# Experts' stage with the sum's turn, residual and final norm taken in, and the last expert's down product split first

## The reference

```python
act = glu * sigmoid(1.702 * glu) * (lin + 1.0)
yb  = (act @ w_down[e] + b_down[e]) * p            # per expert, its tokens
y   = segment_sum(yb)                              # back to the 256 tokens
x   = x + g2 * y
x   = x * rsqrt(mean(x * x) + eps) * final_norm_g  # input of the second block
```

## Time and profile before

| | us |
|---|---|
| median of 3 runs | 3181.67 |
| the profiled execution | 3196.83 |
| its span, first to last instruction | 3195.0 |
| mean granted TensorE clock, share of full | 0.924 |

### The profile page before, as it was taken

One profiled execution on the slowest core, in us unless ns is written; L12 is line 12 of the kernel. 1 busy time (PEld: TensorE's weight loads), 2 busy tenths in 40 slices (PEclk: granted clock), 3 DMA queues, 4 the chain that ended last, 5 costly groups with the idle time before them and its releaser, 6 DMA issues. The chain is left out here.

```text
span 3195.0 us, 43577 instructions
## 1 busy us (share of the span) xinstructions
PE 2973.4 (93%) x17000; PEld 2411.1 (75%) x17001; DVE 2093.8 (66%) x3195; ACT 1608.9 (50%) x2237; POOL 143.4 (4%) x175
## 2 busy tenths in 40 slices
PE   7989999989998879999999999999687899988998
PEld 2458888866767867777777777776685799976998
DVE  2135555534455569999999999997573566574565
ACT  0024444432214358788787887875342445432454
POOL 0023233200000000000000000000000000000000
PEclk9889999998988979999999999999895799985999
DMA  7551010012105489999999999995540255530453
GB/s 260 165 89 34 27 40 14 1 49 73 40 1 150 117 314 381 379 379 381 380 383 379 379 380 378 382 382 201 165 131 1 81 174 175 143 109 1 142 183 125
DMA packets 257848, 604.61 MB, mean 189 GB/s; under 512 B 25987, under 2 KB 82538, under 8 KB 257258
## 3 DMA queue, kind: packets, MB, share of 16 engines
q1 hardware_dynamic: 256556, 601.35, 54.5%
q10 hardware_dynamic: 1085, 0.45, 0.1%
HBM read 596.29 MB, written 5.44 MB: 188 GB/s over the span
## 5 line engine op out<-in xcount | busy, mean ns | idle before, releaser
L2026 DVE TENSOR_TENSOR moe_raw_r<-moe_raw,moe_hi 128x2048 fp32r<-128x2048 f32 x320 | 718.7, 2283 | 10.2 <-ACT moe_hi L1959 10.2
L1959 ACT ACTIVATE moe_hi<-moe_raw 128x2048 fp32r<-128x2048 f32 x320 | 599.7, 1908 | 0.5 <-PE banks L1847 0.5
L2750 PE MATMUL banks<-xs_r,w_hi 128*128 128x272 f32 (+1 forms) x1632 | 475.9, 292 | 25.2 <-DVE w_raw_r L3172 16.6
L2754 PE MATMUL banks<-xs_r,w_raw_r 128*128 128x272 f32 (+1 forms) x1632 | 473.2, 290 | 0.0
L2751 PE MATMUL banks<-xs_r,w_hi 128*128 128x272 f32 (+1 forms) x1632 | 471.0, 289 | 0.0
L2994 ACT ACTIVATE w_hi<-w_raw 128x512 fp32r<-128x512 f32 (+1 forms) x416 | 256.8, 619 | 247.1 <-PE banks L2754 203.4
L2750 PEld LDWEIGHTS banks<-xs_r,w_hi 128*128 128x128 f32 x1632 | 311.9, 191 | 30.3 <-issue 22.3
L2754 PEld LDWEIGHTS banks<-xs_r,w_raw_r 128*128 128x128 f32 x1632 | 312.0, 191 | 3.0
L2751 PEld LDWEIGHTS banks<-xs_r,w_hi 128*128 128x128 f32 x1632 | 312.3, 191 | 0.2
L3172 DVE TENSOR_TENSOR w_raw_r<-w_raw,w_hi 128x512 fp32r<-128x512 f32 (+1 forms) x416 | 271.1, 674 | 57.7 <-ACT w_hi L2994 53.6
L1886 PEld LDWEIGHTS banks<-con,gu_tok 128*128 128x128 f32 x1024 | 191.8, 193 | 30.1 <-ACT gu_tok L1971 9.8
(11 more groups left out here) (484 smaller groups left out, 5523.3 us busy)
## 6 DMA issues: line engine op xcount, KB each, us to landing
moe_raw<-in_w_gu SPq DMA_DIRECT2D x256, 1024.0 KB, 8.4
moe_raw<-in_w_down SPq DMA_DIRECT2D x128, 1024.0 KB, 10.4
w_raw<-in_w_ff SPq DMA_DIRECT2D x256, 256.0 KB, 3.0
w_raw<-in_w_in SPq DMA_DIRECT2D x112, 256.0 KB, 2.7
ring_mod<-in_w_mod SPq DMA_DIRECT2D x12, 2048.0 KB, 8.1
wq<-in_w_in SPq DMA_DIRECT2D x32, 512.0 KB, 4.2
wh<-in_w_in SPq DMA_DIRECT2D x8, 1024.0 KB, 9.5
mg_raw<-in_w_in SPq DMA_DIRECT2D x32, 256.0 KB, 3.0
```

Of the source, the lines that this page charges most:

```text
L1959: act.activation(hi[n % HI_SLOTS][:, :], raw[n % UNITS][:, :], ACT.Copy).then_inc(his, 1)
L2026: dve.tensor_tensor(rest[n % UNITS][:, :], raw[n % UNITS][:, :], hi[n % HI_SLOTS][:, :].bitcast(F32), ALU.subtract).then_inc(los, 1)
L2750: pe.matmul(bank, w_hi, x[:, 0, 0:n_cols], start=first, stop=False)
L2754: ins = pe.matmul(bank, w_lo, x[:, 0, 0:n_cols], start=False, stop=last)
```

## The change

All that the three stages did moves into the experts' stage, behind the last expert:
- The last expert's four units of its down product are rounded and subtracted in one go, on ScalarE ahead of the up sums, on VectorE ahead of `act_first(0)`.
- `scatter` goes through its four products in another order (column half first, token half second) for every expert; in the last one each of the four raises the semaphore.
- The sums are taken out in four parts, two by ScalarE and two by VectorE, each as its product ends; they are turned as before. VectorE adds the residual straight from the turned sums in PSUM, so `yT` and its copies go. The squares go to another buffer (`sum_f`).
- The squares' sum, and the scaling of it, are made ahead of the rare path. Each engine reads the flag earlier (VectorE before the scatter, ScalarE behind the squares, TensorE behind its sum, SyncE behind its last load) and jumps, where no expert overflows, behind that. The rare path itself adds its part to x with a product of its own, and then makes the squares and their sum anew.
- The root's table is loaded behind the squares. A new semaphore `settled`, raised by VectorE behind its jump, releases the root.
- There is one stage end in place of four, with 64 semaphores of its own and 13 held.

The diff, cut to what runs here:

```diff
@@ names of the stage @@
+                 "scat o_hot ... o_act_v o_squared o_summed o_var o_settled y_out_act y_out_dve y_turned fin1_res fin1_sq fin1_sum "
+                 "fin1_var fin1_settled fin1_std fin1_inv " + " ".join(f"o_w{u}" for u in range(UNITS)))
+        def flag_of(eng):
+            return eng.value_load(flags[0:1, 0:1], min_val=0, max_val=NJ)
+
+        def further(eng, some, body):
+            with eng.If(some > 0):
...
+            def last_pe(pe):
+                for i in range(4):
+                    t, c = i % 2, i // 2
+                    pe.wait_ge((out_act, out_dve)[t], c + 1)
+                    for m in range(4):
+                        k = 4 * c + m
+                        ins = pe.transpose(ps[k // 2][:, k % 2 * LAT + t * P:k % 2 * LAT + (t + 1) * P],
+                                           ytok[:, t, k * P:(k + 1) * P], ident)
+                        if t and m % 2:
+                            ins.then_inc(y_turned, 1)
+                pe.wait_ge(res, 2)
+                for k in range(KT):
+                    pe.wait_ge(squared, k + 1)
+                    ins = pe.matmul(ps[0][:, 0:LAT], ones, sq[:, k, :], start=(k == 0), stop=(k == KT - 1))
+                ins.then_inc(summed, 1)
+                some = flag_of(pe)
+                pe.wait_ge(var, 1)
+                further_pe(pe, some)
+
+            def last_act(act):
+                for c in range(2):
+                    act.wait_ge(scat, NEXP + 2 * c)
+                    act.activation(ytok[:, 0, c * 512:(c + 1) * 512], ps[4 + c][:, :], ACT.Copy).then_inc(out_act, 1)
+                for k in range(KT):
+                    act.wait_ge(res, k + 1)
+                    act.activation(sq[:, k, :], xT[:, k, :], ACT.Square).then_inc(squared, 1)
+                some = flag_of(act)
+                act.preload_act_table(ACT.Sqrt)
+                act.wait_ge(var, 1)
+                further_act(act, some)
+                act.wait_ge(settled, 1)
+                act.activation(rinv, rinv, ACT.Sqrt).then_inc(std, 1)
+
+            def last_dve(dve):
+                some = flag_of(dve)
+                for c in range(2):
+                    dve.wait_ge(scat, NEXP + 2 * c + 1)
+                    dve.tensor_copy(ytok[:, 1, c * 512:(c + 1) * 512], ps[6 + c][:, :]).then_inc(out_dve, 1)
+                for k in range(KT):
+                    dve.wait_ge(y_turned, k // 2 + 1)
+                    dve.scalar_tensor_tensor(xT[:, k, :], ps[k // 2][:, k % 2 * LAT:(k % 2 + 1) * LAT], modT[:, 5 * KT + k, 0:1],
+                                             xT[:, k, :], ALU.mult, ALU.add).then_inc(res, 1)
+                dve.wait_ge(summed, 1)
+                dve.tensor_scalar(rinv, ps[0][:, 0:LAT], 1.0 / D, EPS, ALU.mult, ALU.add).then_inc(var, 1)
+                dve.wait_ge(var, 1)
+                further_dve(dve, some)
+                dve.sem_inc(settled, 1)
+                dve.wait_ge(std, 1)
+                dve.reciprocal(rinv, rinv).then_inc(inv, 1)
...
@@ SyncE, behind its last load @@
+                some = flag_of(sp)
+                sp.wait_ge(res, KT)
+                further_sp(sp, some)
@@ scatter @@
-                        t, c = i // 2, i % 2
-                        ins = pe.matmul(ps[4 + i][:, :], pickTs[e % 2][:, t * P:(t + 1) * P], y[:, c * 512:(c + 1) * 512],
+                        t, c = i % 2, i // 2
+                        ins = pe.matmul(ps[4 + 2 * t + c][:, :], pickTs[e % 2][:, t * P:(t + 1) * P], y[:, c * 512:(c + 1) * 512],
-                        if i == 3:
+                        if i == 3 or e == NEXP - 1:
@@ ScalarE, last expert @@
+                    if not nxt:
+                        for q in range(4):
+                            rounded(d0 + q)
+                        out("u", e)
+                        gated(e, 0)
+                        gated(e, 1)
+                        continue
@@ VectorE, last expert @@
+                    if not nxt:
+                        lo(d0, d0 + 1, d0 + 2, d0 + 3)
+                        for h in range(2):
+                            act_first(e, h)
+                            act_second(e, h)
+                        continue
@@ removed: the stages yt, rare path and fin1 (L2078 to L2316) @@
```

More of the change, by code:

```diff
@@ L1779, in experts @@
         hi.append(last_hi)
+        sq = sum_f[:, :].rearrange("p (k t) -> p k t", k=KT)
         pick = sb("pick", [P, 2, 2, 2, 2 * SLOTS], FR)
@@ L1791, in experts @@
         gcur = sb("gate_cur", [P, 2])
+        ytok, rinv = gs, y[:, 0:LAT]
         fold = con[:, K_FOLD:K_FOLD + SLOTS]
@@ new lines, in experts @@
+                 "o_gt_out o_y_out o_sc_mm o_added o_act_v o_squared o_summed o_var o_settled y_out_act y_out_dve y_turned fin1_res fin1_sq fin1_sum "
+                 "fin1_var fin1_settled fin1_std fin1_inv " + " ".join(f"o_w{u}" for u in range(UNITS)))
[3 more added lines that the diff above has]
+            with eng.If(some > 0):
+                with eng.Fori(E_N, NJ) as j:
+                    number = eng.value_load(flags[0:1, bass.ds(j, 1)], min_val=0, max_val=NJ)
+                    with eng.If(number > 0):
+                        item = eng.value_load(items[0:1, bass.ds(j, 1)], min_val=0, max_val=NJ)
+                        body(item, j - E_N if RMAX == 2 else j % E_N, j)
@@ L1951, in _ @@
                         scatter(e)
+                last_pe(pe)
             @block.scalar
@@ L2019, in _ @@
                 results(NEXP - 1)
+                last_act(act)
             @block.vector
@@ L2076, in _ @@
                 dve.wait_ge(x_kept, 32)
[L2078 to L2110, removed]
@@ L2284, in experts @@
-        sq = raw[0][:, :].rearrange("p (k t) -> p k t", k=KT)
-        rinv = y[:, 0:LAT]
-        with stage(nc, "fin1_res fin1_sq fin1_sum fin1_var fin1_std fin1_inv") as (block, res, squared, summed, var, std, inv):
-            @block.vector
-            def _(dve):
-                for k in range(KT):
-                    dve.scalar_tensor_tensor(xT[:, k, :], yT[:, k, :], modT[:, 5 * KT + k, 0:1], xT[:, k, :], ALU.mult, ALU.add)\
-                       .then_inc(res, 1)
-                dve.wait_ge(summed, 1)
-                dve.tensor_scalar(rinv, ps[0][:, 0:LAT], 1.0 / D, EPS, ALU.mult, ALU.add).then_inc(var, 1)
-                dve.wait_ge(std, 1)
-                dve.reciprocal(rinv, rinv).then_inc(inv, 1)
-                dve.wait_ge(res, KT)
-                dve.wait_ge(inv, 1)
-                for k in range(KT):
-                    dve.scalar_tensor_tensor(xT[:, k, :], xT[:, k, :], vec[:, V_FIN + k:V_FIN + k + 1], rinv,
-                                             ALU.mult, ALU.mult)
-            @block.scalar
-            def _(act):
-                act.preload_act_table(ACT.Sqrt)
-                for k in range(KT):
-                    act.wait_ge(res, k + 1)
-                    act.activation(sq[:, k, :], xT[:, k, :], ACT.Square).then_inc(squared, 1)
-                act.wait_ge(var, 1)
-                act.activation(rinv, rinv, ACT.Sqrt).then_inc(std, 1)
-            @block.tensor
-            def _(pe):
-                for k in range(KT):
-                    pe.wait_ge(squared, k + 1)
-                    ins = pe.matmul(ps[0][:, 0:LAT], ones, sq[:, k, :], start=(k == 0), stop=(k == KT - 1))
-                ins.then_inc(summed, 1)
@@ L2319, in route @@
+                last_dve(dve)
 def route(nc, a, ps, con, vec, xT, modT, ident, ones, h_hi, h_lo, rankr, gate, flags, items, first_units):
```

312 lines of the change are left out of this document (162 added, 150 removed).

## The result

The changed kernel takes 3165.96 us (median of 6 runs, 3163.46 to 3173.54), the kernel before 3182.31 in the same comparison (3180.73 to 3186.85). The ratio is 0.995, with a 95% interval of 0.9937 to 0.9963: 12 to 20 us less. The forecast was 13.8 us less, 3168 us. A second comparison gave 3165.8 us and 0.9949 (0.9931 to 0.9967).

What follows compares the result with a forecast made beforehand. From the last expert's scatter each step waits for the one before, engines mostly idle. That stretch falls from 32.97 to 20.35 us (12.6), plus 1.2 in the last expert: 13.8 less, 3168 us, range 3162 to 3177.

Steps and rivals of the forecast that it cites:

- The tail: From the last expert's scatter start to the second block's first VectorE copy: 32.97 us would fall to 20.35.
- Full clock in the sum: TensorE's squares' sum runs at full clock, 0.43 us a step, keeps pace with the squares and ends at 9.0 us.
- its first rival: Half clock in the squares' sum and no clock gain in the down product: 3.4 + 0.6 us back, 3172 us; chance 0.15.
- The stage end: The one end behind the norm, with 20 semaphore clears on VectorE, costs 3.3 us.
- the line: Cost of a stage end on VectorE: 0.67 us and 0.13 more for each semaphore clear.
- The flag: Jump over the rare path on VectorE and ScalarE, between scaling and root: 2.0 us; TensorE's jump 6.4 us, hidden.
- the rival of the free jump: VectorE's jump nearly free, its code at hand; TensorE's jump then sets the end, 1.2 us sooner: 3166.7 us; chance 0.10.
- The last expert: From its first turn to the scatter: activation and down products start sooner, a gain of 1.2 us.
- the prediction's sign: TensorE's down product in the last expert starts 0.8 us behind its turns, not 2.0.
- I take 1.2, as it came back behind each restart here: Last expert's down products: full clock returns as long after the restart as before, so the whole 1.2 us is gained.
- the other value given, 0.6: Last expert's gain in us if TensorE's full clock came back at its old place.
- The slower rival: Second block draws more half clock after starting about 14 us sooner; 60 us more would give 3198 us; chance 0.05.

Runs made afterwards that it cites:

- turn_old: Changed kernel with sums copied out by ScalarE behind the whole scatter, turned sums copied to yT, residual added from there: 3176.2 us, ratio 0.997.
- before_norare: Kernel before without flag, jump and rare-path body, its stage and 31 clears kept: 3177.3 us, ratio 0.9976.
- after_norare: Changed kernel without the rare path, its flag and its jumps: 3162.5 us, ratio 0.9927.
- before_last: Kernel before with only the last expert's new order added: ratio 0.9994 (0.9979 to 1.0009).
- after_lastold: Changed kernel with the last expert's old order put back: 3171.4 us, ratio 0.9964.

## Why the prediction was right, point by point

- **The number**: 13.8 us forecast, 16.4 measured (12 to 20), 3168 against 3165.96 us. The sign, the size and the range held.
- **The tail**: 12.6 forecast, 13.92 in the trace. Two parts of it were tested: the sums taken out by parts and the residual from PSUM (4.2, turn_old), and flag and jump (4.7 before, 0.7 after, so 4.0: before_norare and after_norare). The rest is read from rows and was not tested part by part. The stage ends were 1.79, 2.96 (the two in the middle, from before_norare) and 0.93 in place of 3.13: 2.55 less. From the residual's start to the sum's end it was 7.27 in place of 4.77: 2.5 less, by overlap and by the sum's clock. From the scatter's start to the residual, without the stage end, it was 9.22, and 8.60 in turn_old: 0.6 less. Together that is 13.9.
- **Full clock in the sum** was right, and its first rival falls: 3.69 us in every trace in which TensorE came to the sum without idle time, and in turn_old behind 2.85 us of it. Behind 5.80, 5.90, 10.61 and 10.64 us of idle time it took 5.38, 6.43, 6.17 and 5.56. One sign was missed: the sum ended 1.09 us behind the last square and not within 0.7.
- **The stage end** was right within 0.2 us, and the line holds from 2 to 28 clears on VectorE at 0.12 to 0.13 each; at 28 it gives 4.3, and 4.09 was measured. One premise was wrong without weight in the sum: there are not as many clears before as after, but 72 (19 on VectorE) before and 77 (20) after.
- **The flag was mis-sized**, the largest error of the tail: 2.0 for the jump on VectorE and ScalarE, and 0.80 measured, of which the jump is 0.64. I read the three blocks on q14 as something the engines had waited for. They came behind the root in the changed kernel, and none came between the scaling and the root. That is the rival of the free jump, though at 0.64 it isn't free. That rival's other half was wrong: TensorE's jump did not set the end, since it takes 3.6 us and not 6.4. What I leaned on is the section Instruction fetch mechanics of the page Runtime: NRT & Kernel Launch of the Trainium skill: a taken jump out of the blocks at hand waits for a fetch. For VectorE and ScalarE I misapplied it, since no fetch stands ahead of their restart. On TensorE a block did come 1.3 us into the jump of 3.6, so the trace agrees that there was a fetch; but the engine restarted 2.3 us behind it, and that part is not explained.
- **The last expert**: in before_last the start of the down product moved by 1.23 as forecast, and in all repeats it lay 0.78 us behind the turns, as the prediction's sign has it (1.81 in the changed kernel's first trace). The step that failed is "I take 1.2, as it came back behind each restart here". In the repeats 0.67 was left, nearer to the other value given, 0.6. The changed kernel's first trace has 1.18 by another way: its turns ran at full clock (3.79 in place of 5.56), and the last subtraction became what `act_first(0)` waited for. That it met the 1.2 is luck.
- **The slower rival** did not come. But the second block's length does move by up to 8.6 us between traces, together with its clock, which is over half of the gain, and the prediction had no term for it on the good side.

## What stays open

The medians fell by 16.4 and 18.1 us, the places account for 14.6 (13.9 and 0.7). The difference is within the intervals. That the last expert's order, worth 0.7 us in its place, goes with 5.6 us between medians, that turn_old lies 10 us higher for 4.2 us of tail, and that two idle microseconds more don't cost two, would fit a second block whose clock depends on when it starts. Against a firm tie to the kernel stands that the executions of after_lastold fall on both sides. With one trace for most kernels it can't be told, and it stays open. Why TensorE restarts 2.3 us behind its block of instructions is open too.

## What to carry to other kernels

A stage end with full meetings costs twice. One cost is its own time (here 0.67 us and 0.12 for each clear). The other is the overlap that it forbids: the 2.5 us between residual and sum, part of it clock, and what of turn_old's 4.2 comes of taking the sums out while the scatter runs. Put a data-dependent jump where the engine with the longest jump (here TensorE, 3.6 us) has nothing that others wait for. Its length is read from when that engine restarts, not from when a block of instructions arrives. When a gain of 0.5% is taken from two traces, compare the place and not the spans: 31 us of difference in span held 15 us of change.

## What the hardware showed that I had not expected

- The jump over the rare path took 0.64 us on VectorE and ScalarE, with no block of instructions fetched in it, and 3.6 on TensorE, of which 2.3 lie behind the block's arrival.
- Behind such a jump ScalarE loaded its table again for a square (1.28 us), for which it loaded none where the squares stood ahead of the jump. Whether the chip or the making of the program asks for that load, no run shows.
- The same 5968 products of the second block took 925 to 934 us of span, and the longer ones had the lower granted clock (0.86 against 0.87 of the whole block), in kernels whose code there is identical.
- One clear of a semaphore costs 0.12 to 0.13 us at a stage end, the same from 2 to 28 of them on an engine.
